# A hybrid transformer layer on one core: when the transposes of normed keys are issued, the order of two reductions and a copy, and the number of idle matmuls at the start

## What is computed

```python
h  = rmsnorm(x, g_mix);  proj = h @ w_in      # q, k, v, forget logits, LRU inputs, memory q, gates
mk, mv = split(rmsnorm(mem, g_mem) @ w_mem_kv, 2)
qm = rmsnorm(mq per head of 256, g_q_mem);  km = rmsnorm(mk per head of 256, g_k_mem)
y_mem = softmax(qm @ km.T / 16) @ mv
q, k = rmsnorm(per head of 128);  y_fox = forgetting_attention(q, k, v, log_f)   # 8 heads
y_lru = rg_lru(conv(lx)) * gelu(lg)
x = x + (sum over branches of sigmoid(gates) * (y_branch @ w_branch)) @ w_out
x = x + conv_geglu(rmsnorm(x)) @ w_ffn_down
```

## Time and profile before

| what | value |
|---|---|
| median of 3 runs | 1636.09 us (1635.90 to 1636.34) |
| the profiled execution, its own time | 1637.33 us |
| span of the profiled execution | 1635.6 us |
| TensorE matmul busy | 1623.1 us (99% of the span) |
| TensorE weight load busy | 1392.8 us (85%) |
| VectorE busy | 1051.1 us (64%) |
| ScalarE busy | 869.9 us (53%) |
| mean granted TensorE clock | 0.999 |

### The profile page before, as it was taken

The page is one execution under the profiler, slowest core; times in us unless marked ns, Lnnn a source line. Parts: engine busy times, 40 slices in busy tenths (PEclk is TensorE's granted clock), DMA queues, the critical chain, the costliest instruction groups (busy, mean ns, idle before and its releaser), DMA issues.

```text
span 1635.6 us, 24812 instructions
## 1 busy us (share of the span) xinstructions
PE 1623.1 (99%) x8560; PEld 1392.8 (85%) x8560; DVE 1051.1 (64%) x1257; ACT 869.9 (53%) x1192; POOL 25.4 (2%) x30
## 2 busy tenths in 40 slices
PE   9999999999999999999999999999999999999999
PEld 7778888778888888888888888888888888888887
DVE  6855578656557466565655777777777777544443
ACT  7565667456555445544544655555555555433332
POOL 0000021000000000000000000000000000000000
PEclk9999999999999999999999999999999999999999
DMA  9544455665455555555555455555555555665663
GB/s 348 181 156 154 148 169 198 230 207 166 158 180 185 190 187 193 185 191 190 182 195 188 163 199 195 189 182 203 180 181 204 192 184 188 205 207 193 206 206 116
DMA packets 85280, 309.58 MB, mean 189 GB/s; under 512 B 9832, under 2 KB 10352, under 8 KB 84976
## 3 DMA queue, kind: packets, MB, share of 16 engines
q1 hardware_dynamic: 83952, 303.14, 54.9%
q0 software_dynamic: 1136, 5.78, 1.1%
q10 hardware_dynamic: 144, 0.01, 0.0%
HBM read 306.78 MB, written 2.11 MB: 189 GB/s over the span
## 4 chain that ended last, share of the span: by engine, by line
PE 96%; DVE 2%; DMA 1%; ACT 1%; issue 0%; SPq 0%; ACTq 0%; DVEq 0%
PE psG L360 93%; PE psM L360 2%; DMA raw<-w_units 1%; DVE W L1018 0%; PE psM L445 0%; ACT W L663 0%; DMA par_sb<-par 0%; DVE normed L1056 0%; PE psM L599 0%; DVE X L1202 0%; PE psM L481 0%; DVE x_n L1298 0%; ACT fox_square L692 0%; PE psM L479 0%; DVE dec_u L1165 0%
## 5 line engine op out<-in xcount | busy, mean ns | idle before, releaser
L1018 DVE TENSOR_TENSOR W<-raw,W 128x1024 fp32r<-128x1024 f32 x566 | 686.7, 1226 | 390.0 <-ACT W L663 387.6
L360 PE MATMUL psG<-X,W 128*128 128x512 f32 (+1 forms) x4864 | 848.5, 336 | 0.0
L360 PEld LDWEIGHTS psG<-X,W 128*128 128x128 f32 x4864 | 741.2, 188 | 104.1
L663 ACT ACTIVATE W<-raw 128x1024 fp32r<-128x1024 f32 x566 | 589.9, 1054 | 400.4 <-PE psG L360 387.1
L360 PE MATMUL psG<-W,hidden 128*128 128x512 f32 x1056 | 239.5, 389 | 0.0
L360 PEld LDWEIGHTS psG<-W,hidden 128*128 128x128 f32 x1056 | 198.1, 188 | 41.1
L360 PE MATMUL psG<-W,X 128*128 128x512 f32 x768 | 180.4, 394 | 0.0
L360 PEld LDWEIGHTS psG<-W,X 128*128 128x128 f32 x768 | 144.5, 189 | 30.2 <-issue 0.3
L671 ACT ACTIVATE low<-psG 128x512 f32<-128x512 f32 x100 | 59.8, 598 | 148.9 <-PE psG L360 148.9
L360 PE MATMUL psG<-Y,W 128*128 x768 | 133.3, 335 | 0.0
L360 PEld LDWEIGHTS psG<-Y,W 128*128 128x128 f32 x768 | 117.0, 188 | 16.0
(11 more groups left out here) (191 smaller groups left out, 551.5 us busy)
## 6 DMA issues: line engine op xcount, KB each, us to landing
raw<-w_units SPq DMA_DIRECT2D x566, 512.0 KB, 3.4
xs<-xT SPq DMA_DIRECT2D x4, 512.0 KB, 8.7
x_tok<-x_rows POOLq DMA_DIRECT2D x1, 2048.0 KB, 13.3
mem_raw<-first_data SPq DMA_DIRECT2D x3, 512.0 KB, 5.0
mem_raw<-memT SPq DMA_DIRECT2D x3, 512.0 KB, 7.4
out<-x_tok POOLq DMA_DIRECT2D x3, 512.0 KB, 4.1
lru_rg<-w_rg POOLq DMA_DIRECT2D x8, 128.0 KB, 4.1
c_all<-c_rows POOLq DMA_DIRECT2D x1, 1024.0 KB, 7.7
```

The lines of the kernel that those rows point to most:

```text
L360: return nc.tensor.matmul(*a, skip_group_check=True, **kw)
L663: nc.scalar.activation(W[:, s, :, 0], raw[:, s], ACT.Copy).then_inc(hi_done, 1)
L1018: V.tensor_tensor(W[:, s, :, 1], raw[:, s], f32(W[:, s, :, 0]), ALU.subtract).then_inc(lo_done, 1)
```

## The change

A table `TURN_UNIT` gives, for each of the eight turns, the unit of the next group behind which TensorE transposes: 3 for the two groups of memory keys, 2 for kq2 (j = 6), 1 as before for the other five. ScalarE's copy of the turned result moves with it, to the unit last+5+n (n = 1 is last+6, as before). The adds for x's sums begin at unit 16 instead of 15, so that the pair at `first`+2 and the last pair stand behind the copies of the memory values. The idle matmuls at the start are nine instead of seven.

```diff
+TURN_UNIT = [3, 3, 1, 1, 1, 1, 2, 1]
...
-            for _ in range(7):
+            for _ in range(9):
                 mm(psM[:, 3, 0:P], ones[:], ones[:], start=True, stop=True)
...
-            wide_group("mk", 1, m_op, {1: turn(0)})
+            wide_group("mk", 1, m_op, {TURN_UNIT[0]: turn(0)})
...
-            wide_group("mq", 0, x_op, {1: turn(1)}, ready=x_ready)
+            wide_group("mq", 0, x_op, {TURN_UNIT[1]: turn(1)}, ready=x_ready)
...
-            wide_group("kq", 3, x_op, {1: turn(6, act=side_count("fox", 0, "act", "weights_copied")), **attention_hooks("fox", 1)})
+            wide_group("kq", 3, x_op, {TURN_UNIT[6]: turn(6, act=side_count("fox", 0, "act", "weights_copied")), **attention_hooks("fox", 1)})
...
             starts = {"normed": [last + 1 for last in (GROUPS[g][3] for g in NORM_GROUP)],
+                      "turned": [GROUPS[g][3] + 5 + n for g, n in zip(NORM_GROUP, TURN_UNIT)],
...
-            steps_at = {"normed": {3: [norm_squares], 5: [turned_copied]}, "mem": softmax, "fox": softmax,
+            steps_at = {"normed": {3: [norm_squares]}, "turned": {0: [turned_copied]}, "mem": softmax, "fox": softmax,
...
-                for first, n in ((11, "mem"), (15, "x")):
+                for first, n in ((11, "mem"), (16, "x")):
```

More of the change, by code:

```diff
@@ L556, in _ @@
             wide_group("mk", 0, m_op, {0: mem_sums, 4: x_sums})
-            wide_group("mk", 1, m_op, {1: turn(0)})
+            wide_group("mk", 1, m_op, {TURN_UNIT[0]: turn(0)})
             x_ready = lambda n: pe.wait_ge(xX_lo, n // 2 + 1)
-            wide_group("mq", 0, x_op, {1: turn(1)}, ready=x_ready)
-            wide_group("mq", 1, x_op, {1: turn(2), **attention_hooks("mem", 0)})
-            plain("lru", None, {1: turn(3, act=side_count("mem", 0, "act", "weights_copied")), **attention_hooks("mem", 1)})
+            wide_group("mq", 0, x_op, {TURN_UNIT[1]: turn(1)}, ready=x_ready)
+            wide_group("mq", 1, x_op, {TURN_UNIT[2]: turn(2), **attention_hooks("mem", 0)})
+            plain("lru", None, {TURN_UNIT[3]: turn(3, act=side_count("mem", 0, "act", "weights_copied")), **attention_hooks("mem", 1)})
             with pe.Fori(1, 4) as i:
@@ L566, in _ @@
             wide_group("kq", 0, x_op, {})
-            wide_group("kq", 1, x_op, {1: turn(4, dve=side_count("decay", 0, "dve", "z"))})
-            wide_group("kq", 2, x_op, {1: turn(5), **attention_hooks("fox", 0)})
-            wide_group("kq", 3, x_op, {1: turn(6, act=side_count("fox", 0, "act", "weights_copied")), **attention_hooks("fox", 1)})
-            plain("gate0", None, {1: turn(7, act=side_count("fox", 1, "act", "weights_copied")), **attention_hooks("fox", 2)})
+            wide_group("kq", 1, x_op, {TURN_UNIT[4]: turn(4, dve=side_count("decay", 0, "dve", "z"))})
+            wide_group("kq", 2, x_op, {TURN_UNIT[5]: turn(5), **attention_hooks("fox", 0)})
+            wide_group("kq", 3, x_op, {TURN_UNIT[6]: turn(6, act=side_count("fox", 0, "act", "weights_copied")), **attention_hooks("fox", 1)})
+            plain("gate0", None, {TURN_UNIT[7]: turn(7, act=side_count("fox", 1, "act", "weights_copied")), **attention_hooks("fox", 2)})
             plain("gate0", 1, attention_hooks("fox", 3))
```

## The result

The changed kernel takes 1627.55 us (median of 4 runs, 1627.46 to 1629.60) against 1636.21 us before (4 runs, 1635.90 to 1638.86): 8.7 us less, ratio 0.9949 with a 95% interval of 0.9937 to 0.9961. The forecast was 1629.0 (1626.9 to 1631.8). The profiled execution fell from 1637.33 to 1627.56 us, its span from 1635.6 to 1625.8.

A forecast was written before the change was run, and what follows sets the result against it. TensorE, busy 99% of the span, bounds the kernel, so only its waits and slow clock count. Waits of 2.5 + 2.3 + 0.7 = 5.5 us plus one clock term of 1.6: 1636.09 - 7.1 = 1629.0 us, range 1626.9 to 1631.8.

The forecast's parts named there:

- The waits of turns 0 and 1: TensorE's waits for the norm before these turns' transposes go when moved two units later: 2.5 and 2.3 us won.
- rival (c): TensorE waits for splits near units 28 to 30 instead; only 0.7 us remain, 1635.4 us; chance 0.07, whole or part.
- (d): Slower: the moved copy at unit 31 holds ScalarE and the split of unit 32, 1639.4 us; chance 0.03.
- The drop behind turn 1: Half-speed clock for some 3.4 us after turn 1's wait goes with that wait: 1.6 us, bounds 0 and 1.6.
- About one of the two clock terms: Main case: waits plus 1.6 us for one of the drop behind turn 1 and the start, 1629.0 us; chance 0.40.
- rival (b): Both clock terms, behind turn 1 and at the start, are won: 1627.5 us, at most 1626.9; chance 0.23.
- The start: Two more idle matmuls make the first ten real matmuls faster: 1.5 us, 6 in 10, bounds 0 and 2.1.
- The sums: At unit 16, adds of x's sums moved behind the memory values' copy end TensorE's wait for it: 0.7 us.
- Turn 6: Moved from behind unit 121 to behind 122, where there was no wait: costs and gives nothing.
- Turn 4: TensorE's wait of 1.50 us at this turn stays.
- the prediction's theory of the short gap: At the start, shrinking the idle gap before real work from 1.24 to about 0.3 us may raise the clock earlier.

The follow-up runs named there:

- experiment 9: The kernel before with only turns 0 and 1 moved behind unit 3 of the next group, seven idle matmuls, sums at unit 15: 1630.15 us.
- experiment 2: The changed kernel with all turns behind unit 1 again, sums and nine idle matmuls kept: 1635.26 us over 11 runs.
- experiment 1: The changed kernel with seven idle matmuls again instead of nine: 1629.27 us (1627.81 to 1630.20).
- experiment 5: The kernel before with only turn 1 moved, behind unit 35, and its ScalarE copy with it: 1633.25 us over 10 runs.
- experiment 10: The kernel before with only x's sums moved, to begin at unit 16: 1634.60 us over 11 runs, ratio 0.9993.
- experiment 3: The changed kernel with x's sums beginning at unit 15 again: 1629.51 us (1628.89 to 1629.76).
- experiment 4: The kernel before with nine idle matmuls instead of seven and nothing else: 1635.73 us over 11 runs, ratio 0.9999.
- experiment 6: The changed kernel with turn 6 back behind unit 121: 1627.52 us (1627.21 to 1627.92).
- experiment 7: The changed kernel with turn 4 moved too, from behind unit 105 to behind unit 106: 1626.34 us (1626.13 to 1626.42).

## Why the prediction was right, and where it was not

**The waits of turns 0 and 1: right in mechanism and size.** 4.8 us with a drop of 1.6 were expected; experiment 9, which moves just these two, gives 6.4. Undone in the changed kernel they cost 7.7 us (experiment 2), since there most runs have a drop behind both turns. Covers turned out as worked out (3.1 for 3.3 us at turn 0), and no split was waited for, so rival (c) has nothing behind it. Nor has (d): the moved ScalarE copy runs at 86.06 without holding TensorE.

**The drop behind turn 1: right to count, and the choice against it was wrong.** The prediction doubted it for the timed runs, since the median lay 1.2 us under the profiled time. In 50 timed runs of the kernel before, on the chips of the experiments, 39 have a mean clock of 0.999 (median 1636.3), 7 of 0.998 (1638.0) and 4 of 1.000 (1635.2). As far as the mean clock tells (three of the seven at 0.998 are as fast as those at 0.999), one drop was the rule. The 1.2 us between the profiled execution and the median say nothing on it: the runs at 0.999 alone spread from 1635.3 to 1637.2. "About one of the two clock terms" was therefore the step that failed: both were won (1.6 us behind turn 1, 1.8 at the start), which is rival (b), forecast at 1627.5 with a chance of 0.23. The point forecast was 1.5 us too high, about the size of that term. That (b) meets the median so closely is partly luck: its 8.6 us were taken from the median, while the span of the profiled executions fell by 9.8, with 0.5 us at turn 4, 0.3 more at the start and 0.14 for the first matmul that no term held.

**The start: right in size, wrong as a term of its own.** It was put at 1.5 of at most 2.1 us; in the profiles it was 1.8, and 1.7 by experiment 1. What was missed is how far the moment of the rise varies with seven idle matmuls. The packed traces hold the granted clock as records with a time, and the first record stands where the spacing of the matmuls falls to 0.23 us for 512 columns (or to 0.11 for the idle ones). With seven idle matmuls it stands at 4.20 us in experiment 5, 8.69 and 8.89 in experiments 9 and 10, 10.43 in the kernel before and 10.63 in experiment 1; with nine at 4.09 to 6.75 in seven profiles; with eleven at 5.76. The Trainium skill ("TensorE: Matmul & The Clock Gate", Part 1) says that the count of slow matmuls varies from run to run. The traces agree for both counts, but nine keep the rise early, so the rule was no reason to set the term to 0. One timed run of the changed kernel, 1629.60 us at a mean clock of 1.000, lies 2.0 us above the other three; it left no profile, so a slow start with nine can't be excluded.

**The sums: the term that was mis-sized.** It was put at 0.7 us, with the wait's length read from a run with a slow start. Undone in the changed kernel it costs 2.0 us (experiment 3). The prediction worked out the cover of each edit against the schedule of before and not against the one that the other edits make: an earlier TensorE lengthens a wait for work whose time is set by the weight loads, ScalarE and VectorE. The same holds the other way: the start alone is worth 0.5 us or less (experiment 4), since the wait at unit 16 takes 1.0 us of it and the clock some of the rest. The whole came out right all the same because in the changed kernel both edits are made, so that neither wait is left.

**Turn 6 is worth nothing,** as forecast (experiment 6). **Turn 4** was expected to stay at 1.50 us and stands at 1.04 in the changed kernel; in the seven-idle kernel of experiment 1 it was 0.69. In the kernel before, the chain to this wait goes back to a load of weights that landed at 332.08 us; in the two others it goes back through ScalarE's split to TensorE, and no load stands in it. Why it is 1.04 in one and 0.69 in the other is open. Moving the turn takes it away whole (experiment 7).

## What to carry to other kernels

In a kernel bound by one engine, list that engine's waits and ask for each how far behind its releaser the consumer could be moved: one unit of 2.7 us was enough here. A wait costs its length, and one of about 2 us cost in some executions 1.6 us more for the clock behind it, so remove such a wait even where the one profile shows no drop. And size an edit against the schedule that the other edits of the same change will make: one that removes a wait of 0.6 us today may be the one that lets 2 us from elsewhere through.

## What the runs showed of the hardware

In the 13 profiles, TensorE waited ten times for 1.89 to 2.33 us, and behind six of these waits the granted clock fell to its lower level for about 3.4 us. Behind turn 0's 2.3 us it fell in experiments 2 and 4, but not in the kernel before, experiment 5 or 10; behind turn 1's 2.11 us in the kernel before, experiments 2 and 4, but not in 10; behind 1.89 us at unit 16 in experiment 5. Behind waits of 1.28, 1.56 and 1.77 us at unit 16 (experiments 9, 4 and 3) and of up to 1.50 us at turn 4 it never fell. So it differs between kernels with the same wait and, by the mean clocks of experiment 2, between executions of one kernel; what decides it is open.

The mean granted clock of a run, 1.000, 0.999 or 0.998, counts the drops only roughly. One drop, 3.4 us at half speed, takes 0.001 off it and costs 1.6 us, and in experiment 2 the runs sort by it. But two runs of experiment 10 at 0.999 lie 4.0 us apart (1632.94 and 1636.91). One thing that blurs the count: the clock also falls when TensorE's work is over, within the span: in the changed kernel's profile the last matmul ends at 1622.15 us, and the stretch from 1624 to 1625 us has 0.83.

The column of the granted clock does not show the slow start. In the profile of experiment 1 it reads 1.00 from the first microsecond, while the matmuls last 628 ns:

```profile
7.00:8.00 1.00, 1.00 (x3) 1.00 1.03 422
8.00:9.00 1.00, 1.00 (x4) 1.00 1.00 381
...
11.00:12.00 1.00, 1.00 (x6) 1.00 1.01 410
```

The first record of the clock in this trace is at 10.63 us; before it there is none, and the view shows 1.00. At the start of a kernel, read the durations and the counts, not the clock column.

Why the rise comes when it does was not settled. In experiments 3, 4 and 5 the clock was up (4.55, 4.09 and 4.20 us) before the last idle matmul had ended and the gap of 1.1 to 1.3 us began, so their fast starts say nothing on what a gap does. Where the clock was still low when real work began, it rose 0.5 to 1.2 us later behind gaps of 0.24 to 0.41 us (the changed kernel, experiments 6 and 7, nine idle matmuls), and 3.0 to 5.3 us later behind gaps of 0.90 to 1.29 us (the kernel before, experiments 1, 9 and 10, seven). That fits the prediction's theory of the short gap, but the gap and the number of idle matmuls change together in these runs, and no run separates them.
